# The dense down stage as one unrolled stream of 66 chunks, with deeper buffers and sums marked bank by bank

## The reference, cut to what matters

```python
def swiglu(h, w_g, w_u, w_d):
    return (jax.nn.silu(h @ w_g) * (h @ w_u)) @ w_d
...
        if l % 2 == 0:
            x = x + g2 * swiglu(h, ffn_w_gate[i], ffn_w_up[i], ffn_w_down[i])
            if ctx_out:
                hc = modulate(rmsnorm(xc, norm_ffn_g[l]), csh2, csc2)
                xc = xc + cg2 * swiglu(hc, ffn_w_gate[i], ffn_w_up[i], ffn_w_down[i])
```

## Time and profile before

| | us |
|---|---|
| median of 3 timed runs | 6105.13 |
| the three runs | 6094.68 to 6106.96 |
| the profiled execution, its own time | 6100.45 |
| its span, from first to last instruction | 6098.5 |

### The profile page before, as it was taken

The page is one execution under the profiler, slowest core; times in us unless marked ns, Lnnn a source line. Parts: engine busy times, 40 slices in busy tenths (PEclk is TensorE's granted clock), DMA queues, the critical chain, the costliest instruction groups (busy, mean ns, idle before and its releaser), DMA issues. The chain is left out here.

```text
span 6098.5 us, 61033 instructions
## 1 busy us (share of the span) xinstructions
PE 5281.8 (87%) x22972; PEld 3997.5 (66%) x22973; DVE 2772.0 (45%) x2881; ACT 2003.3 (33%) x1980; POOL 163.6 (3%) x239
## 2 busy tenths in 40 slices
PE   6899395699997969967576999999999999999994
PEld 2444174588886744425465888877887888887883
DVE  0220474311113332126524644699558644448566
ACT  1100111211112220011112534577447534437453
POOL 0000020000000000001101000000000000000001
PEclk8899697799998989978786999999999999999996
DMA  9111003211215431010227755699669755558575
GB/s 377 29 43 54 15 1 136 84 56 60 63 35 183 136 131 36 14 64 1 90 104 297 297 186 199 242 365 367 228 224 355 275 186 200 199 186 333 200 264 220
DMA packets 262623, 996.66 MB, mean 163 GB/s; under 512 B 40000, under 2 KB 112384, under 8 KB 175744
## 3 DMA queue, kind: packets, MB, share of 16 engines
q1 hardware_dynamic: 243200, 926.43, 41.4%
q0 software_dynamic: 13040, 49.29, 2.2%
q10 hardware_dynamic: 6288, 19.66, 0.8%
HBM read 911.68 MB, written 83.63 MB: 163 GB/s over the span
## 5 line engine op out<-in xcount | busy, mean ns | idle before, releaser
L1696 PE MATMUL ps<-moe_gate_up_hi,moe_xh 128*128 128x512 f32 x2464 | 964.9, 392 | 29.1 <-DVE moe_gate_up_lo L1841 29.1
L1696 PE MATMUL ps<-moe_gate_up_hi,moe_xl 128*128 128x512 f32 x2464 | 962.9, 391 | 0.0
L1696 PE MATMUL ps<-moe_gate_up_lo,moe_xh 128*128 128x512 f32 x2464 | 962.6, 391 | 0.0
L1841 DVE TENSOR_TENSOR moe_gate_up_lo<-moe_wst,moe_gate_up_hi 128x2048 fp32r<-128x2048 f32 x424 | 952.8, 2286 | 20.1 <-ACT moe_gate_up_hi L1774 20.1
L1774 ACT CAST moe_gate_up_hi<-moe_wst 128x2048 fp32r<-128x2048 f32 x424 | 792.1, 1922 | 0.0
L1854 DVE TENSOR_TENSOR moe_down_lo<-moe_wst,moe_down_hi 128x2048 fp32r<-128x2048 f32 x210 | 480.6, 2292 | 165.3 <-ACT moe_down_hi L1788 165.3
L1696 PEld LDWEIGHTS ps<-moe_gate_up_hi,moe_xh 128*128 128x128 f32 x2464 | 465.4, 189 | 128.3 <-DVE moe_gate_up_lo L1841 31.4
L1696 PEld LDWEIGHTS ps<-moe_gate_up_hi,moe_xl 128*128 128x128 f32 x2464 | 464.9, 189 | 97.3
L1696 PEld LDWEIGHTS ps<-moe_gate_up_lo,moe_xh 128*128 128x128 f32 x2464 | 465.3, 189 | 96.5
L1860 DVE TENSOR_TENSOR moe_a<-moe_sil,ps 128x512 f32<-128x512 f32 x210 | 143.9, 685 | 753.6 <-ACT moe_sil L1794 753.6
L1794 ACT ACTIVATE moe_sil<-ps 128x512 f32<-128x512 f32 x210 | 126.0, 600 | 1032.2 <-PE ps L1696 1032.0
(11 more groups left out here) (329 smaller groups left out, 6497.9 us busy)
## 6 DMA issues: line engine op xcount, KB each, us to landing
moe_wst<-in_moe_packed SPq DMA_DIRECT2D x634, 1024.0 KB, 6.7
ada_w<-in_ada_packed SPq DMA_DIRECT2D x24, 2048.0 KB, 26.5
down_wst<-in_ffn_w_down SPq DMA_DIRECT2D x66, 512.0 KB, 3.6
proj_w<-in_w_in SPq DMA_DIRECT2D x8, 2048.0 KB, 7.9
four_dft<-in_dft_seq SPq DMA_DIRECT2D x16, 1024.0 KB, 4.9
xs_d<-route_zero SPq DMA_DIRECT2D x1, 16384.0 KB, 51.8
moe_rows<-xs_d POOLq DMA_DIRECT2D x16, 1024.0 KB, 5.6
ys_d<-moe_y POOLq DMA_DIRECT2D x15, 1024.0 KB, 8.5
```

Source lines behind the costliest of these rows:

```text
L1696: x = nc.tensor.matmul(ps[:, 2 * (q % 2) + i, :], xx[:, k, t], w[:, q % 2, k, :], start=(k == 0 and j == 0), stop=(k == KD - 1 and j == 2))
L1841: nc.vector.tensor_tensor(gul[:, q % 2, k, :], wst[:, slot(n), :].rearrange("p (k n) -> p k n", k=4), guh[:, q % 2, k, :].bitcast(F32), AL ...
```

## The change

The down stage is written as one straight stream of 66 steps, numbered c, on every engine, without loops. There are four staging buffers (`RING`) and three buffers of parts (`PARTS`). What the steps compute is the same.

- SP no longer loads all of `x` first. It loads the four first chunks at once, and later chunk c when chunk c-4 has been split. `x` is loaded group by group, each time behind the loads of the chunk f = 8 of the group. The stores of group g-1 are issued behind it, in two halves of 4 blocks, and those of the last group at the end. ACT issues no DMA any more.
- PE marks a new semaphore, `summed`, once per bank in the last chunk of a group, and `used` in the others.
- ACT waits for the parts buffer of chunk c-3.
- DVE splits the first two chunks of the next group (f = 0 and 1) before it makes the sums of a group, and each sum waits for its own bank.

```diff
--- before.py
+++ after.py
@@ -1319,96 +1319,93 @@
 def phase_ffn_down(nc, io, S):
 
     NC = DFF // P
+    RING, PARTS = 4, 3
+    chunks = [(g, f) for g in range(len(GROUPS)) for f in range(NC)]
     with Phase(nc, "down") as ph:
-        wst = ph.sb("wst", [P, 2, D])
-        wh = ph.sb("wh", [P, 2, D], F32R)
-        wlo = ph.sb("wl", [P, 2, D], F32R)
-        ast = ph.sb("ast", [P, 2, 512])
-        ah = ph.sb("ah", [P, 2, 512], F32R)
-        alo = ph.sb("al", [P, 2, 512], F32R)
+        wst = ph.sb("wst", [P, RING, D])
+        ast = ph.sb("ast", [P, RING, 512])
+        wh = ph.sb("wh", [P, PARTS, D], F32R)
+        wlo = ph.sb("wl", [P, PARTS, D], F32R)
+        ah = ph.sb("ah", [P, PARTS, 512], F32R)
+        alo = ph.sb("al", [P, PARTS, 512], F32R)
         x = ph.sb("x", [P, KD, T])
-        wl = [ph.sem(f"loaded{s}") for s in range(2)]
-        hi, split, used, added, xl, st = (ph.sem(n) for n in ("hi_ready", "split", "used", "added", "x_loaded", "stored"))
+        wl = [ph.sem(f"loaded{s}") for s in range(RING)]
+        xl = [ph.sem(f"x_loaded{g}") for g in range(len(GROUPS))]
+        hi, split, used, summed, added, st = (ph.sem(n) for n in ("hi_ready", "split", "used", "summed", "added", "stored"))
         ps, mod = S["ps"], S["mod"]
-
-        def over_chunks(eng, chunk, g):
-
-            for s in range(2):
-                chunk(0, s, g, s == 0, False)
-            with eng.Fori(1, NC // 2 - 1) as i:
-                for s in range(2):
-                    chunk(i, s, g, False, False)
-            for s in range(2):
-                chunk(NC // 2 - 1, s, g, False, s == 1)
-
         with nc.Block() as block:
 
             @block.sync
             def _(sp):
-                sp.dma_start(x[:, :, :], S["xT_d"]).then_inc(xl, 16)
-
-                def load(i, s, g, first, last):
+                def store(g, half):
                     t0, n = GROUPS[g]
-                    sp.wait_ge(split, i * 2 + (g * NC + s + 1))
-                    sp.dma_start(wst[:, s, :], io["ffn_w_down"][0][bass.ds(i * 256 + s * P, P), :]).then_inc(wl[s], 16)
-                    sp.dma_start(ast[:, s, :n], S["a_d"][:, bass.ds(i * 2 + s, 1), t0:t0 + n].rearrange("p a t -> p (a t)")).then_inc(wl[s], 16)
-
-                for g in range(3):
-                    over_chunks(sp, load, g)
+                    sp.wait_ge(added, KD * g + 4 * half + 4)
+                    sp.dma_start(S["xT_d"][:, 4 * half:4 * half + 4, t0:t0 + n], x[:, 4 * half:4 * half + 4, t0:t0 + n]).then_inc(st, 16)
+
+                for c, (g, f) in enumerate(chunks):
+                    t0, n = GROUPS[g]
+                    if c >= RING:
+                        sp.wait_ge(split, c - RING + 1)
+                    sp.dma_start(wst[:, c % RING, :], io["ffn_w_down"][0][f * P:(f + 1) * P, :]).then_inc(wl[c % RING], 16)
+                    sp.dma_start(ast[:, c % RING, :n], S["a_d"][:, f, t0:t0 + n]).then_inc(wl[c % RING], 16)
+                    if f == 8:
+                        sp.dma_start(x[:, :, t0:t0 + n], S["xT_d"][:, :, t0:t0 + n]).then_inc(xl[g], 16)
+                        if g:
+                            for half in range(2):
+                                store(g - 1, half)
+                for half in range(2):
+                    store(len(GROUPS) - 1, half)
+                sp.wait_ge(st, 16 * 2 * len(GROUPS))
 
             @block.tensor
             def _(pe):
-                pe.sem_inc(used, 2)
-
-                def products(i, s, g, first, last):
-                    n = GROUPS[g][1]
-                    pe.wait_ge(split, i * 2 + (g * NC + s + 3))
+                for c, (g, f) in enumerate(chunks):
+                    n, s = GROUPS[g][1], c % PARTS
+                    pe.wait_ge(split, c + 1)
                     for d in range(KD):
-                        if first and g:
+                        if f == 0 and g:
                             pe.wait_ge(added, KD * (g - 1) + d + 1)
                         for j, (w, aa) in enumerate(((wh, ah), (wh, alo), (wlo, ah))):
                             mm = nc.tensor.matmul(ps[:, d, :n], w[:, s, d * P:(d + 1) * P], aa[:, s, :n],
-                                                  start=(first and j == 0), stop=(last and j == 2))
-                    mm.then_inc(used, 1)
-
-                for g in range(3):
-                    over_chunks(pe, products, g)
+                                                  start=(f == 0 and j == 0), stop=(f == NC - 1 and j == 2))
+                        if f == NC - 1:
+                            mm.then_inc(summed, 1)
+                    if f < NC - 1:
+                        mm.then_inc(used, 1)
 
             @block.scalar
             def _(act):
-
-                def parts_hi(i, s, g, first, last):
-                    n = GROUPS[g][1]
-                    act.wait_ge(wl[s], i * 32 + (16 * g * NC + 32))
-                    act.wait_ge(used, i * 2 + (g * NC + s + 1))
-                    nc.scalar.copy(wh[:, s, :], wst[:, s, :])
-                    nc.scalar.copy(ah[:, s, :n], ast[:, s, :n]).then_inc(hi, 1)
-
-                for g in range(3):
-                    over_chunks(act, parts_hi, g)
-                for g, (t0, n) in enumerate(GROUPS):
-                    act.wait_ge(added, KD * (g + 1))
-                    act.dma_start(S["xT_d"][:, :, t0:t0 + n], x[:, :, t0:t0 + n]).then_inc(st, 16)
-                act.wait_ge(st, 48)
+                for c, (g, f) in enumerate(chunks):
+                    n, s = GROUPS[g][1], c % PARTS
+                    act.wait_ge(wl[c % RING], 32 * (c // RING + 1))
+                    if c >= PARTS:
+                        gb, fb = chunks[c - PARTS]
+                        if fb == NC - 1:
+                            act.wait_ge(summed, KD * (gb + 1))
+                        else:
+                            act.wait_ge(used, gb * (NC - 1) + fb + 1)
+                    nc.scalar.copy(wh[:, s, :], wst[:, c % RING, :])
+                    nc.scalar.copy(ah[:, s, :n], ast[:, c % RING, :n]).then_inc(hi, 1)
 
             @block.vector
             def _(dve):
-                dve.sem_inc(split, 2)
-
-                def parts_lo(i, s, g, first, last):
-                    n = GROUPS[g][1]
-                    dve.wait_ge(hi, i * 2 + (g * NC + s + 1))
-                    nc.vector.tensor_tensor(wlo[:, s, :], wst[:, s, :], wh[:, s, :].bitcast(F32), ALU.subtract)
-                    nc.vector.tensor_tensor(alo[:, s, :n], ast[:, s, :n], ah[:, s, :n].bitcast(F32), ALU.subtract).then_inc(split, 1)
-
-                for g, (t0, n) in enumerate(GROUPS):
-                    over_chunks(dve, parts_lo, g)
-                    dve.wait_ge(used, NC * (g + 1) + 2)
-                    dve.wait_ge(xl, 16)
+                def sums(g):
+                    t0, n = GROUPS[g]
                     j = 1 if t0 < CTX else 0
+                    dve.wait_ge(xl[g], 16)
                     for d in range(KD):
+                        dve.wait_ge(summed, KD * g + d + 1)
                         nc.vector.scalar_tensor_tensor(out=x[:, d, t0:t0 + n], in0=ps[:, d, :n], scalar=mod[:, 0, 40 + d, j:j + 1],
                                                        in1=x[:, d, t0:t0 + n], op0=ALU.mult, op1=ALU.add).then_inc(added, 1)
+
+                for c, (g, f) in enumerate(chunks):
+                    n, s = GROUPS[g][1], c % PARTS
+                    dve.wait_ge(hi, c + 1)
+                    nc.vector.tensor_tensor(wlo[:, s, :], wst[:, c % RING, :], wh[:, s, :].bitcast(F32), ALU.subtract)
+                    nc.vector.tensor_tensor(alo[:, s, :n], ast[:, c % RING, :n], ah[:, s, :n].bitcast(F32), ALU.subtract).then_inc(split, 1)
+                    if g and f == PARTS - 2:
+                        sums(g - 1)
+                sums(len(GROUPS) - 1)
 
 
 def phase_route(nc, io, S, hT, R):
```

## The result

| | before | after |
|---|---|---|
| median of the timed runs, us | 6101.79 (4 runs, 6094.68 to 6106.96) | 6056.31 (4 runs, 6049.99 to 6058.98) |
| the profiled execution, us | 6100.45 | 6054.69 |
| its span, us | 6098.5 | 6053.1 |

The ratio is 0.9925, with a 95% interval of 0.9908 to 0.9942: 45.5 us faster, against the 46.8 us forecast, and within 1 us of the forecast time.

What follows compares the result with a forecast made beforehand. PE was taken as the engine to keep fed in the down stage; 12.6 + 12.6 + 5.5 + 9.4 + 6.7 = 46.8 us off 6102.8 gave 6056, with 6044 to 6070 for the likeliest case.

Steps and rivals of the forecast that it cites:

- Start: Before the down stage's first matmul: chunk 0's weights go first instead of 5 MB of `x`; gain 12.6 us, bounds 9.6 to 13.2.
- Group 0: Its 21 later chunks run at PE's pace, 2.93 us each, 61.5 instead of 74.10; gain 12.6 us, bounds 8 to 13.6.
- The slack of 4.0 us: Group 0's four-buffer ring: a load lands 7.7 us after chunk k-3 ends and is wanted at 11.7 us.
- First border: Between groups 0 and 1: PE stands 1.3 us and the slow chunk goes, where 6.81 us were lost; gain 5.5 us.
- Second border: Behind chunk 43: PE does not stand at all and the next chunk keeps full clock; gain 9.4 us.
- End: Last matmul's start to next phase's load: 7.8 instead of 14.46 us, storing in halves; gain 6.7, bounds 2.0 to 8.4.
- Costs set to nothing: Down stage: bank waits on DVE, stores and loads of `x` in groups 1 and 2, and straight code cost nothing.
- a stage elsewhere that changes its length: Sign of a wrong forecast: a stage outside the down stage gets longer or shorter; no size given.
- the loads bound group 0: Rival, 10%: with four loads in flight landings take longer, 3.5 us per chunk; 12 us of gain go, 6068.
- the slower rival: Rival, 2%: long landings make the ring starve PE in every group; 6100, or 6144 at a landing of 20 us.
- At the ends: Rival, 3%: first landing of the stage at 6.8 us and last at 9.6 give 8 us back; 6064.
- idle time without a cause: Sign of the instruction supply rival, 3%: PE's loop-free code waits for instruction packets, 38 us; 6094.

## Why the prediction was right, point by point

- **Start:** forecast 12.6 us, measured 12.5 (7.42 instead of 19.90; first matmul forecast at 7.3). The first activations landed 4.0 us after their issue, near the 3.8 taken.
- **Group 0:** forecast 12.6, measured 13.6 for the 21 later chunks, since a chunk took 2.88 us, my lower bound, not 2.93: the 47 intervals of the earlier trace rows included the one after an idle time, which is 0.1 us longer. The first chunk gave 0.5 us too, which I had at nothing. The reason was right, the ring: loops alone gave nothing, and with two staging buffers the gain of group 0 was gone. The slack of 4.0 us until ACT wants a load was about right (3.5 to 4.4 us for chunks 12 to 21 of the changed kernel, 0.9 us behind the load of `x`), but PE has another 2.5 us behind it, which I had left out.
- **First border:** forecast 5.5 with a stand of 1.3, measured a stand of 1.34 and a gain of 5.4; the chunk behind it ran at 1.00, as forecast.
- **Second border:** forecast 9.4, measured 9.4.
- **End:** forecast 6.7, measured 7.2. Of the 7.8 us forecast as 1.4 + 4.9 + 1.5, 7.28 came as 1.21 to the issue, 4.2 to the landing and 1.9 to the next load: the half landed faster than I took it, and what follows was slower.
- **Costs set to nothing:** the loads and stores of `x` inside groups landed slowly and were hidden, as argued. From issue to landing, min/median/max, of the stores and of the loads of `x` in the changed kernel (compare):

```profile
DMA to landing us min/median/max: 4.2/11.8/14.4
...
DMA to landing us min/median/max: 8.1/10.3/10.3
```

  Straight code cost nothing: group 0 ran 506 matmuls in 60.48 us without a gap.
- **The sum:** 46.8 forecast for the stage, 48.6 measured. Each term was within 1.0 us, but for the first chunk's 0.5 that I had left out.

The total was right in part by luck, since errors cancelled. The stage gave 48.6 us; the experts' stage gave 7.7 back. The two profiles of each kernel differ by 44.5 us on average (6100.45 and 6099.38; 6054.69 and 6056.16). Of the other 3.6 us, 3.0 lie ahead of the stage, which began at 1836.74 and 1835.69 before and at 1832.55 and 1833.96 after, and the rest outside both stages. The 3.0 are spread: in the ten other runs the stage began between 1831.79 and 1836.72, whatever the kernel. The prediction named the give-back only as "a stage elsewhere that changes its length", among its signs of being wrong and with no price. That sign came. A step that would have priced it: look in the other stages for stands of some us between dense matmuls, and allow the slow stretch behind each of them, 1.8 us here, either way. What decides for a program whether the clock falls behind these stands is open. The length of the straight code alone doesn't explain it (the written-out loops had the shortest experts' stage), and moving one load gave the longest.

The rivals fell. Group 0 ran at PE's pace although its activations landed later than before (4.2 us after their issue in the median, not 3.5); with only two staging buffers the loads bound group 0 and the first border, never groups 1 and 2, so the slower rival was far off. At the ends the landings were 4.0 and 4.2 us, not 6.8 and 9.6. No idle time without a cause appeared in the straight code, while the page counts nine instruction packets more than the earlier trace rows:

```profile
q8 instruction: 70, 1.15, 0.1%
```

## What to carry to other kernels

Cut the stage at the gaps of its limiting engine and price each gap by the row that ends it; five such prices added up to within 2 us of 48.6. A ring is deep enough if a load is never later than its own slack plus the time that the next engine's operands lie ready (2.5 us here in group 0). Count both, and buffers can be saved: three and three would have done here, at 0.4 us. A stand of the limiting engine at a border can cost more than its length: 1.7 us of clock behind each stand of 2.6 here, nothing behind stands up to 1.3. So let the next group's first operands be made before the last group's sums.

## What the runs showed of the hardware that I had not expected

- TensorE's clock fell behind stands of 2.6 us in the middle of dense work (7.17 us for a chunk of 5.44, granted clock 0.76), and behind one of 3.07 us with two staging buffers (5.28 us for a chunk of 2.88, granted clock 0.50), while stands of 1.0 to 1.3 us left it at 1.00.
- Behind stands of the same 2.8 and 3.4 us the clock fell in one program (0.66 to 0.81 over the next 8 us) and stayed at 1.00 in another, alike in both profiles of each program. That moved a stage with unchanged code by 7.7 us, and between 2714.4 and 2728.0 us over all kernels.
- One issue of a DMA on SP took 2.77 and 3.30 us behind three loads of 5 MB in all made of short rows (256 or 512 columns of 8 blocks); behind one load of the same 5 MB in long rows it took 0.42. Whether the rows or the number of loads makes the difference was not tested.
